# Expert slots, a sort in two native fp32 halves, and matmuls of constants beside the router

## The reference

```python
x = x + merged @ w_out
h = rmsnorm(x, norm2_g)                       # (320, 1024)
g_prob = softmax(h @ w_router_group + b); g_p, g_idx = top_k(g_prob, 1)
e_prob = softmax(logits of that group's 8 experts); e_p, e_idx = top_k(e_prob, 2)
e_p = e_p / sum(e_p)
combine = onehot(g) * onehot(e) * e_p * g_p   # (320, 32), two entries a row
for each of 32 experts:
    hg = silu(h @ w_gate[e]) * (h @ w_up[e])  # width 256
    out += (hg * combine[:, e]) @ w_down[e]
return x + out
```

## Time and profile before

| what | value |
|---|---|
| median of three runs | 878.8 us |
| profiled execution | 872.89 us, span 871.4 us |
| PE busy | 750.2 us, 86% |
| DVE busy | 401.8 us, 46% |
| ACT busy | 298.5 us, 34% |
| POOL busy | 144.1 us, 17% |
| mean DMA rate over the span | 233 GB/s |
| DMA on the chain that ended last | 17% |

### The profile page before, as it was taken

How to read it: one execution, slowest core, us unless ns; L and a number is a source line. 1 busy time by engine, 2 the same in 40 slices (tenths; PEclk the granted TensorE clock), 3 DMA queues, 4 the chain that set the end, 5 groups by cost and what they waited for, 6 DMA issues and landing times.

```text
span 871.4 us, 14531 instructions
## 1 busy us (share of the span) xinstructions
PE 750.2 (86%) x5476; PEld 597.2 (69%) x5476; DVE 401.8 (46%) x936; ACT 298.5 (34%) x550; POOL 144.1 (17%) x245
## 2 busy tenths in 40 slices
PE   2999899998888999997968799986589999787780
PEld 1899899996555699996857689985555555444440
DVE  3575333466544456584445547764752222111123
ACT  5433553655333255663221224544221111111110
POOL 5001000002333200103222300001212222112210
PEclk9999999999899999999989999998699999999995
DMA  5245233226677642727565625984579999999986
GB/s 184 97 146 181 101 142 139 104 97 213 173 232 219 194 146 103 255 97 237 140 206 168 191 93 189 347 344 171 224 318 418 417 419 418 419 418 419 418 322 190
DMA packets 38170, 202.84 MB, mean 233 GB/s; under 512 B 7490, under 2 KB 8018, under 8 KB 18898
## 3 DMA queue, kind: packets, MB, share of 16 engines
q1 hardware_dynamic: 24434, 160.29, 48.1%
q0 software_dynamic: 13664, 41.58, 15.3%
HBM read 184.24 MB, written 23.38 MB: 238 GB/s over the span
## 4 chain that ended last, share of the span: by engine, by line
PE 59%; DMA 17%; DVE 11%; ACT 5%; issue 5%; SPq 1%; POOLq 1%; POOL 1%; DVEq 0%; ACTq 0%
PE bank L1694 20%; PE bank L1698 9%; DMA fm<-in_w_moe 7%; DMA em<-in_w_moe 7%; PE bank L2042 6%; PE bank L1684 3%; PE bank L1850 3%; PE bank L2062 3%; DMA fm<-in_cache_lf 2%; DVE rm L1104 2%; PE bank L1899 2%; ACT rm L781 2%; PE bank L2023 2%; PE bank L1839 1%; PE bank L1934 1%
## 5 line engine op out<-in xcount | busy, mean ns | idle before, releaser
L1694 PE MATMUL bank<-rm 128*128 128x320 f32 x1344 | 207.5, 313 | 2.6 <-ACT fm L809 1.6
L1694 PEld LDWEIGHTS bank<-rm 128*128 128x128 f32 x1344 | 199.0, 189 | 7.4 <-issue 3.9
L1104 DVE TENSOR_TENSOR rm<-fm,rm 128x2048 fp32r<-128x2048 f32 x48 | 110.0, 2293 | 69.5 <-ACT rm L781 69.0
L1698 PE MATMUL bank<-rm 128*128 128x256 f32 x960 | 122.4, 286 | 2.4 <-DVE fm L1474 2.4
L1698 PEld LDWEIGHTS bank<-rm 128*128 128x128 f32 x960 | 118.4, 194 | 3.2 <-issue 2.9
L2044 PE MATMUL bank<-fm,em 128*64 128x256 f32 x384 | 98.1, 401 | 0.0
L781 ACT ACTIVATE rm<-fm 128x2048 fp32r<-128x2048 f32 x48 | 91.9, 1915 | 17.8 <-PE bank L1694 11.2
L2042 PE MATMUL bank<-em 128*64 128x256 f32 x272 | 66.7, 389 | 9.8 <-DMA fm<-in_w_moe 6.4
L2042 PE MATMUL bank<-fm,em 128*64 128x256 f32 x240 | 61.7, 404 | 12.2 <-DMA fm<-in_w_moe 10.8
L2042 PEld LDWEIGHTS bank<-em 128*64 128x64 f32 x272 | 35.6, 138 | 36.5 <-issue 21.9
L1067 ACT ACTIVATE fm<-bank 64x256 f32<-64x256 f32 x32 | 12.0, 376 | 136.3 <-PE bank L2044 136.3
(11 more groups left out here) (387 smaller groups left out, 1013.3 us busy)
## 6 DMA issues: line engine op xcount, KB each, us to landing
fm<-in_w_moe SPq DMA_DIRECT2D x57, 1024.0 KB, 27.6
fm<-in_w_dense SPq DMA_DIRECT2D x48, 1024.0 KB, 4.9
em<-in_w_moe SPq DMA_DIRECT2D x39, 1024.0 KB, 27.7
fm<-in_state_C POOLq DMA_DIRECT2D x32, 257.0 KB, 4.4
out_C_sample<-fm POOLq DMA_DIRECT2D x32, 257.0 KB, 5.3
fm<-in_cache_kT POOLq DMA_DIRECT2D x16, 512.0 KB, 5.0
fm<-in_cache_v POOLq DMA_DIRECT2D x16, 512.0 KB, 4.5
fm<-y_rows SPq DMA_DIRECT2D x4, 512.0 KB, 5.3
```

Source lines behind the costliest of these rows:

```text
L1104: s(TT(pair[c % 2][1], cube(raw[c % RAW1], KC), pair[c % 2][0], ALU.subtract), sem("split_done"))
L1694: ins = mm(bank[b][:, 0:NT], w[:, k, P * u:P * (u + 1)], a[:, k, :], start=first, stop=final)
L1698: ins = mm(bank[b][0:r, 0:CW], a[:, k, TILE0[u]:TILE0[u] + r], w[:, k, :], start=first, stop=final)
```

## The change

Five things change, all between the last dense matmul and expert 3.

1. h2 is no longer split. The sort multiplies h2 and the one-hot matrix in native fp32 (three matmuls of 320 columns to a half chunk); ACT's high copies and POOL's three subtractions are gone.
2. The sort is in two halves of 320 slots. The first half (all 8 chunks) comes before the experts, as the sort did. The first five experts' starts are clamped so that their 64 slots lie in it. The second half is sorted by PE behind down(1) (chunks 0 to 3) and behind down(2) (chunks 4 to 7), through banks 6 and 7; DVE makes the second half of `onehot` between its copies of the first. POOL waits for it before it packs expert 5.
3. While DVE chooses the experts, PE runs 28 matmuls of `ident` by `ones` into bank 5, whose result nobody reads.
4. The slots. h2 and the router's small tiles, `onehot`, `xe` and `gat` move in memory. Of the 21 slots 18 are free before the sort; loads 18 to 25 then reuse slots 0 to 7, each after its use; loads 26 to 28 go into the three slots that h2, `onehot` and the small tiles held and wait for the whole sort; from 29 on load n waits for the use of load n - 21.
5. DVE's late words move from expert 0 to behind expert 1's copy, and the row table behind down(0).

```diff
-        slot = rawm[8:12] + [halves[8192], halves[8192 + UN], rawm[2], rawm[3], rawm[4], rawm[0], rawm[1],
-                             halves[13312], halves[13312 + UN], halves[13312 + 2 * UN]] + rawm[5:8] + \
-                            [halves[q * UN] for q in range(4)]
+        slot = rawm[8:12] + [halves[8192], halves[8192 + UN]] + rawm[2:6] + [rawm[0], rawm[1], halves[13312],
+                                                                             halves[13312 + UN], halves[13312 + 2 * UN]] + \
+            [halves[q * UN] for q in range(1, 4)] + [rawm[6], halves[0], rawm[7]]
...
+        NSLOT, NFREE, NAGAIN = len(slot), 18, 8
+        HALF, NBEFORE = SLOTS // 2, 5
...
+            if n < NFREE:
+                return n
+            if n < NFREE + NAGAIN:
+                return n - NFREE
+            return n - NAGAIN if n < NSLOT + NAGAIN else slot_of(n - NSLOT)
...
-                elif n == 14:
-
-                    sp.wait_ge(sem("h2T_full"), 2 * CPS)
-                    sp.wait_ge(sem("h2_split"), 3)
-                elif n == 17:
+                elif n == NFREE + NAGAIN:
 
                     sp.wait_ge(sem("sorted_full"), 2 * KC)
-                elif n >= NSLOT:
+                    sp.wait_ge(sem("late_done"), 1)
+                elif NFREE <= n < NFREE + NAGAIN:
+
+                    sp.wait_ge(sem("e_used"), n - NFREE + 1)
+                elif n >= NSLOT + NAGAIN:
 
                     sp.wait_ge(sem("e_used"), n - NSLOT + 1 if n < 3 * NE - 1 else unit(NE - 8, 2) + 1)
...
-            for t in range(3):
-                r = ROWS[t]
-                pool.wait_ge(sem("h2_hi"), t + 1)
-                g(nc.gpsimd.tensor_tensor(h2s[1][:, t, :] if t < 2 else h2s[0][NS:2 * NS, t, :], h2[0:r, t, :],
-                                          h2s[0][0:r, t, :], ALU.subtract), sem("h2_split"))
-
             def packed(v):
 
                 place = pool.value_load(off_i[:, v:v + 1], min_val=0, max_val=SLOTS)
+                if v == NBEFORE:
+                    pool.wait_ge(sem("xs_ready"), 2)
...
+            s(TSC(off_i[:, 1:NBEFORE], offs[0:1, 1:NBEFORE], float(HALF - CAP), None, ALU.min))
...
+            for _ in range(28):
+                mm(bank[5][:, 0:P], ident, ones, start=True, stop=True, skip_group_check=True)
             pe.wait_ge(sem("chosen"), 1)
...
-            def sort(n, t):
-
-                k, half = n // 2, n % 2
-                for i in range(2 if t < 2 else 1):
-                    ins = mm(bank[n % 4][:, 0:NT], h2s[i][:, t, P * k:P * (k + 1)],
-                             onehot[:, t, NT * half:NT * (half + 1)], start=(t == 0 and i == 0), stop=(t == 2))
+            def sort(b, k, half, t):
+
+                r = ROWS[t]
+                ins = mm(bank[b][:, 0:HALF], h2[0:r, t, P * k:P * (k + 1)], onehot[0:r, t, HALF * half:HALF * (half + 1)],
+                         start=(t == 0), stop=(t == 2))
...
+            def sort_more(ks):
+
+                pe.wait_ge(sem("onehot"), 6)
+                for k in ks:
+                    if k >= 2:
+                        pe.wait_ge(sem(("sorted_free_a", "sorted_free_v")[k % 2]), KC // 2 + k // 2)
+                    for t in range(3):
+                        sort(6 + k % 2, k, 1, t)
...
                 down(4 + v % 2, htp[v % 2], weights(v, 2)).then_inc(sem("e_used"), 1)
+                if v == 0:
+                    row_table()
+                elif v in (1, 2):
+                    sort_more(range(4 * (v - 1), 4 * v))
```

More of the change, by code:

```diff
@@ L325, in hybrid_step @@
         offs = take(NE)
-        assert top[0] <= FW
+        blkf = cube(take(NE * JB), NE)
+        assert top[0] <= base_raw + 8 * UN
         squares, lgT = em[:, 12288 + 384:12288 + 384 + CW], em[:, 12288 + 640:13312]
         turn40 = fm[:, base_masks + 1240:base_masks + 1280]
[L329 to L333, removed]
+        top[0] = base_raw + 8 * UN
         crowd_s = [take(D)[0:NS, :] for _ in range(2)]
-        assert top[0] <= base_yrow
+        xe = cube(em[:, UN:UN + 3 * D], 3)
+        gat = [em[:, 13312 + D * i:13312 + D * (i + 1)] for i in range(6)]
         row_of = small[:, 84:90]
@@ L1040, in _ @@
                 r = ROWS[t]
-                s(A_(h2[0:r, t, :], h2[0:r, t, :], ACT.Copy, scale=small[0:r, 9 + t:10 + t]))
-                s(A_(h2s[0][0:r, t, :], h2[0:r, t, :], ACT.Copy), sem("h2_hi"))
+                s(A_(h2[0:r, t, :], h2[0:r, t, :], ACT.Copy, scale=small[0:r, 9 + t:10 + t]), sem("h2_scaled"))
             act.wait_ge(sem("router_args"), 1)
@@ L1049, in _, with sorted_more @@
             act.wait_ge(sem("x1_stored"), 16)
-            for n in range(0, 2 * KC, 2):
-                k, half = n // 2, n % 2
-                act.wait_ge(sem("sorted_full"), n + 1)
-                s(A_(xs[:, k, NT * half:NT * (half + 1)], bank[n % 4][:, 0:NT], ACT.Copy), sem("sorted_free_a"))
+            for k in range(0, KC, 2):
+                act.wait_ge(sem("sorted_full"), k + 1)
+                s(A_(xs[:, k, 0:HALF], bank[k % 4][:, 0:HALF], ACT.Copy), sem("sorted_free_a"))
+            def sorted_more(ks):
+                for k in ks:
+                    act.wait_ge(sem("sorted_full"), KC + k + 1)
+                    A_(xs[:, k, HALF:SLOTS], bank[6][:, 0:HALF], ACT.Copy).then_inc(sem("sorted_free_a"), 1)
             def take_y(v):
@@ L1590, in late_words @@
                 s(CP(flag_i, most[0:1, 0:1]))
-                for j in range(JB):
-                    s(TSC(blkf[0:1, :, j], offs[0:1, :], float(CAP * j), float(SLOTS), ALU.add, ALU.min))
-                s(CP(blk_i, blkf[0:1, :, :].rearrange("p e j -> p (e j)")))
+                s(TSC(blk_i, blkf[0:1, :, :].rearrange("p e j -> p (e j)"), float(SLOTS), None, ALU.min), sem("late_done"))
             def take_y(v):
@@ L2074, in start, with row_table @@
                 last_u.then_inc(sem("e_used"), 1)
-            start(0)
-            pe.wait_ge(sem("onehot"), 3 + 6)
-            for k in range(2):
-                for t in range(3):
-                    i, r = 3 * k + t, ROWS[t]
-                    ins = mm(bank[6][0:CAP, 0:NE], at_rank[i][0:r, :], hot[k][0:r, t, :], start=(i == 0), stop=(i == 5))
-            ins.then_inc(sem("router_full"), 1)
+            def row_table():
+                pe.wait_ge(sem("onehot"), 6 + 6)
+                for k in range(2):
+                    for t in range(3):
+                        i, r = 3 * k + t, ROWS[t]
+                        ins = mm(bank[6][0:CAP, HALF:HALF + NE], at_rank[i][0:r, :], hot[k][0:r, t, :], start=(i == 0),
+                                 stop=(i == 5))
+                ins.then_inc(sem("router_full"), 1)
+            start(0)
             for v in range(NE):
```

89 lines of the change are left out of this document (53 added, 36 removed).

## The result

The changed kernel takes 892.24 us (median, 891.3 to 896.89); the kernel before took 879.32 us on the same chip. The ratio is **1.0164 [1.0115, 1.0214]**: slower, twice as much as forecast and outside the forecast's range. The profiled execution took 892.81 us, its span is 891.3 us (before: 871.4).

What follows compares the result with a forecast made beforehand. The prediction took the DMA stream of expert weights to bound the kernel. Load 26 waits until 666.2, then 70 x 2.595 us gives 847.9 against 840.54: +7.3 us, 886.1 us on the median of before; range 878.5 to 891.

Steps and rivals of the forecast that it cites:

- POOL's split goes, 4.8 us: DVE's choice of experts: stalls beside POOL's subtractions vanish, so the choice ends at 612.1 instead of 616.89; bounds 0 and 4.8.
- 28 matmuls of constants: PE ahead of the count: 8 at 0.44 us, then 20 at 0.22, ending at 614.0, 1.9 us after the choice.
- Sort start: From choice to sort on PE: 3.4 us instead of 4.66, so the sort starts at 617.4, 4.1 us earlier.
- Sort, first half: 13.0 us: PE before the experts: 24 native matmuls of 320 columns at 0.54 us each, until 630.4.
- rival A: PE later still: clock falls between count and sort, constants never raise it, or DVE's stalls stay; 889 us, chance 0.15.
- The evacuations and the store of x1 are hidden: During the first half of the sort: x1 lands about 622.7, first chunk full at 622.3, bank wanted at 623.9.
- From the first use to the end of the sort: 30.9 us: PE from 635.3 through expert work, row table and two 6.5 us groups of four sorted chunks, until 666.2.
- The cover of eight loads and the hole: SP's weight stream: eight reused slots cover 20.8 us, until 656.1; load 26 waits for the sort, DMA idles 10 us.
- 70 x 2.595 us behind it: Weight stream after load 26's wait: 70 remaining loads from 666.2, last landing at 847.9 against 840.54.
- PE's extra 13 us cost nothing by themselves: PE among the experts: the second half's sorting adds no time itself, since later PE waits for weights.
- Rival B: The hole in the weight stream costs little, 0 to 4 us remain; 881 us, chance 0.14.
- rival C: Native sort matmuls run at 0.15 us each, stream nearly continuous, 11 us earlier than before; 868 us, chance 0.07.

Runs made afterwards that it cites:

- Full tiles: Changed kernel with the sort's third row tile (64 rows) replaced by the second tile's 128 rows again; 886.24 us, ratio 1.0136 to the kernel before.
- The three repairs: Changed kernel without the constants, POOL's row-number wait moved behind packing expert 2, second half sorted one expert earlier; 884.49 us, ratio 1.0089.
- POOL's short pieces: Kernel before, with POOL's three split subtractions cut into 24 of 128 columns each, nothing else; 873.34 us, ratio 0.996.
- the halves with the fp32r split: Kernel before with the sort in halves, one-pass fp32r, POOL's split in 12 pieces, 17 free slots, second half behind down(0) and down(1); 877.27 us, ratio 1.0014.

## Why the prediction came out as it did

The direction and the main mechanism were right, the size was not: +7.3 us were forecast; the trace shows 17.8, the timed ratio 10 to 19. The terms that failed are the first half of the sort and the time from the first use to the end of the sort, both too short, and PE's extra work, put at nothing.

- *POOL's split goes, 4.8 us.* Right: choice at +7.4 forecast, +7.3 measured.
- *28 matmuls of constants.* End at +9.3 forecast; the count behind them started at +10.2: the clock rose 5.8 us into them, not 3.4. That they use up DVE's gain held. That PE would then be at the upper level for the sort did not.
- *Sort start.* +12.7 forecast, +13.65 measured, the constants' 0.9.
- *Sort, first half: 13.0 us.* Failed: 16.6 us. Two causes. The clock fell 0.2 us into it, behind the pause of 1.64 us, and stayed at the lower level until 624.0 (rival A's mechanism, 1.7 us by its own arithmetic: 3.4 us at half speed), and the changes between 128 and 64 rows cost 1.76. Full tiles took 14.85 us with the same clock fall.
- *The evacuations and the store of x1 are hidden.* Right; the store took 13.1 us.
- *From the first use to the end of the sort: 30.9 us.* Failed: 37.8 us. The two second halves took 8.1 us each instead of 6.5 (+3.2; full tiles: 6.7). PE waited 1.6 us for POOL's packing of expert 2, and the clock then fell once more to 0.50 for 3.4 us, which costs 1.7: +3.3 in all. 0.4 us are left without a name. I had counted POOL's queue only for expert 5 and its store, not for the wait for row numbers that the moved row table made later.
- *The cover of eight loads and the hole.* The mechanism was right to the row: eight loads, a stop at load 26, DMA at 0.04. The eight kept DMA at a mean share of 0.92 until 666, 24 us behind the first use and not 20.8; the hole is 14 us, not 10. Load 26 was forecast at +61.5 and went at +73.1, 11.6 us later: 0.9 + 3.6 + 6.9, and 0.2 in expert 0's gate and up. What stands behind it took 1.1 us less than forecast (211.4 against 212.5), which leaves the miss of 10.5, 17.8 against 7.3.
- *70 x 2.595 us behind it.* Right: 2.58, both counted to the last landing that the chain waits for, with two loads behind it.
- *PE's extra 13 us cost nothing by themselves.* Wrong, though hidden here behind the hole: with the wait gone, taking away two thirds of the second half's matmuls brought the ratio from 1.0046 to 1.0015 and the trace from 273.7 to 269.4 us.

The three repairs put load 26 at +62.6, near the forecast's place, and the kernel at a ratio of 1.0089; the forecast's +7.3 us are 1.0084. So the sum from load 26 on was sound, and the terms ahead of it were mis-sized. That the repaired kernel meets the forecast's number is partly chance, since it reaches it by sorting one expert earlier. Rival A named one of them at 3 us; its 889 was also too low. Rows 9, which it cites for both levels of the clock, show the lower one and a mean of 0.53; the upper stands in rows 1. Rival B was wrong by the windows, rival C by the matmuls' duration. The fault of the range: I let all uncertainties of PE's path enter as one rival, while they add, each in the same direction, on a path where every microsecond counts fully.

What stays open: why a change between 128 and 64 rows costs PE 0.19 us in native fp32 (only its price is shown), what besides the length of a pause makes the clock fall, what kept half of the lead of POOL's short pieces from the end, and whether the constants' 2 us and the 3.6 us of POOL's wait, both read from single traces, are there in the times, whose intervals are wider.

## What to carry to other kernels

When a queue's wait is moved behind reused slots, work out when the awaited work ends with every engine on the way, queue by queue; the loads that cover it are a fixed budget (here 8 x 2.6 us), and each microsecond beyond it reaches the end in full. Where a short instruction on DVE stalls beside a long one on POOL, cut the long one in pieces before giving up the work itself: that edit alone was worth 0.4% (0.1 to 0.7%), more than any other here. Where matmuls of two tile heights alternate, group those of one height, as the first four chunks did. Work given to PE to keep its clock up must reach to the next real work; here the clock was down again at the start of the sort, behind a pause of 1.6 us, in every trace with that pause.

## What the hardware showed beyond expectation

- Native fp32 matmuls on a full array go by columns, 0.43 us for 256 and 0.54 for 320 at the upper level; with one 64-row tile in three they average 0.67, because each change between the two heights adds 0.19. Four 64-row matmuls in a row cost 0.54 each and one change.
- The granted clock fell in or right behind PE's pause of 1.64 us ahead of the sort in all seven traces that have it, behind 9 us of constants; the lower level then lasted 3.4 us in six of them and 6.8 in one. Behind the pause of 1.6 us at expert 2 it fell in five traces of six, for 3.4 us, and in the sixth (full tiles) it stayed at 1.00. So the pause's length alone does not decide.
- POOL's subtraction of 24 tiles of 128 columns takes 0.61 us a tile start to start, three of 1024 columns 2.4 us each: a short piece costs twice as much a column. Pieces of 256 columns take 0.81 us (12 in 9.67 us, in the halves with the fp32r split).
